# One multiplication and one sum for the dots of four gathered rows, in one group of three

## The reference

```python
qry = (xb @ peer_query).reshape(P, PEER_HEADS, 2, PEER_KEY_DIM)
scores = jnp.einsum('phsd,hsnd->phsn', qry, keys)
top_s, top_i = lax.top_k(scores, PEER_TOPK)
cand = top_s[:, :, 0, :, None] + top_s[:, :, 1, None, :]
best_s, best_c = lax.top_k(cand.reshape(...), PEER_TOPK)
expert = ia * PEER_KEYS + ib            # 16 experts per frame and head
gate = jax.nn.softmax(best_s)
act = jax.nn.gelu(jnp.einsum('pd,ped->pe', xb, peer_down[expert]))
out = jnp.einsum('pe,ped->pd', gate * act, peer_up[expert])
```

## Time and profile before

| | |
|---|---|
| time, median of 3 runs | 1663.01 us (1662.77 to 1663.81) |
| profiled execution, time | 1664.46 us |
| its span, first to last instruction | 1662.7 us |
| busy: TensorE, VectorE, ScalarE, GpSimd | 1383.8, 1174.9, 573.3, 716.7 us |
| DMA | 608.39 MB, mean 366 GB/s |
| mean granted TensorE clock | 0.946 |

### The profile page before, as it was taken

The page is one execution under the profiler, slowest core; times in us unless marked ns, Lnnn a source line. Parts: engine busy times, 40 slices in busy tenths (PEclk is TensorE's granted clock), DMA queues, the critical chain, the costliest instruction groups (busy, mean ns, idle before and its releaser), DMA issues.

```text
span 1662.7 us, 14018 instructions
## 1 busy us (share of the span) xinstructions
PE 1383.8 (83%) x4311; PEld 678.6 (41%) x4311; DVE 1174.9 (71%) x2555; ACT 573.3 (34%) x1785; POOL 716.7 (43%) x633
## 2 busy tenths in 40 slices
PE   7999999998898789778977897789779877777733
PEld 6744465554353335324433443344324423332311
DVE  3997758966876777677767776777777777676755
ACT  3112231632433333333333333333433333333342
POOL 0004624644444445444444444445444444444552
PEclk9999999999899999999999999999999999999955
DMA  7203227999999999999999999999999999999996
GB/s 293 102 1 100 110 77 279 371 421 422 422 420 422 421 422 420 422 421 422 420 422 421 422 421 422 421 421 421 421 422 421 421 422 420 419 420 421 414 421 256
DMA packets 87978, 608.39 MB, mean 366 GB/s; under 512 B 11104, under 2 KB 13664, under 8 KB 16224
## 3 DMA queue, kind: packets, MB, share of 16 engines
q0 software_dynamic: 78336, 570.46, 82.9%
q1 hardware_dynamic: 9568, 37.04, 5.9%
HBM read 604.19 MB, written 2.88 MB: 365 GB/s over the span
## 4 chain that ended last, share of the span: by engine, by line
DMA 44%; PE 37%; DVE 10%; issue 3%; ACT 3%; POOL 2%; DVEq 0%; SPq 0%; POOLq 0%
DMA arena<-experts,expert 44%; PE ps L1686 18%; PE ps L1549 8%; PE ps L1649 5%; DVE arena L1329 4%; PE ps L1529 4%; POOL arena L603 2%; ACT weight L907 1%; ACT late L917 1%; PE ps L1508 1%; DVE cst L1305 0%; DVE cst L1308 0%; DVE picked L1312 0%; PE ps L1620 0%; ACT gl L899 0%
## 5 line engine op out<-in xcount | busy, mean ns | idle before, releaser
L1686 PE MATMUL ps<-arena,late 128*128 128x512 f32 x2016 | 950.3, 624 | 206.0 <-ACT late L917 205.7
L603 POOL DMA_INDIRECT arena<-experts,expert x544 | 645.2, 1186 | 732.4 <-PE ps L1686 627.5
L1329 DVE CUSTOM_DVE_ANT_0 arena<-arena,hn 128x1024 f32<-128x1024 f32 x544 | 656.7, 1222 | 384.9 <-DMA arena<-experts,expert 381.8
L1686 PEld LDWEIGHTS ps<-arena,late 128*128 128x128 f32 x2016 | 387.3, 198 | 745.0 <-issue 450.7
L899 ACT ACTIVATE gl<-dots 128x2 f32<-128x2 f32 (+1 forms) x274 | 55.8, 204 | 814.3 <-DVE dots L1329 814.3
L917 ACT ACTIVATE late<-cst,weight 128x128 f32<-128x128 f32 (+1 forms) x536 | 183.5, 389 | 8.8
L907 ACT ACTIVATE weight<-gl,gate 128x1 f32<-128x1 f32 x544 | 130.7, 287 | 8.9
L1549 PE MATMUL ps<-arena,hT 128*128 128x512 f32 x256 | 112.3, 598 | 0.0
L1649 PE MATMUL ps<-hT,region_b 128*128 128x272 f32 x448 | 106.9, 392 | 0.0
L1649 PEld LDWEIGHTS ps<-hT,region_b 128*128 128x128 f32 x448 | 85.1, 190 | 27.9 <-issue 12.4
L1072 DVE SCALAR_TENSOR_TENSOR region_b<-region_b,par 128x574 f32<-128x574 f32 x120 | 92.5, 813 | 4.5
(11 more groups left out here) (174 smaller groups left out, 872.1 us busy)
## 6 DMA issues: line engine op xcount, KB each, us to landing
arena<-weights SPq DMA_DIRECT2D x6, 2048.0 KB, 11.0
region_b<-head_weights SPq DMA_DIRECT2D x8, 1152.0 KB, 9.5
arena<-experts,expert POOLq DMA_INDIRECT x544, 22.4
hT<-x_turned SPq DMA_DIRECT2D x2, 1088.0 KB, 7.2
arena<-weights SPq DMA_DIRECT2D x4, 512.0 KB, 10.7
xs<-x_prompt SPq DMA_DIRECT2D x4, 512.0 KB, 10.0
arena<-weights SPq DMA_DIRECT2D x2, 1024.0 KB, 13.9
y_prompt<-xs SPq DMA_DIRECT2D x4, 512.0 KB, 3.8
```

Of the source, the lines that this page charges most:

```text
L603: pool.indirect_dma_start(rows_of(n), None, experts, bass.IndirectOffsetOnAxis(ap=expert[:, vt % BUFS, k:k + 1], axis=0))\
L1329: last = v.tensor_tensor_reduce(out=rows_of(n)[:, 0:D], in0=rows_of(n)[:, 0:D], in1=hn[:, tile_of(vt)], scale=1.0, scalar=0.0, op0=ALU.mul ...
L1686: last = mm(ps[:, 2 * (vt % 2) + half, :], diag[:, n % DIAGS, :], rows_of(n)[:, D + half * SEC:D + (half + 1) * SEC], start=k == first * G ...
```

## The change

Three things are changed. The last four slots of `CYCLE` come in the order 10, 11, 8, 9, whose places are 0, 1, 2, 3. `FOURS` lists the groups, between rows 64 and 511, whose four buffers lie side by side in that order: every third group, 38 in all, beginning with row 64, 76, 88 and so on to 508. By visit they are the first and the fourth group of visits 4, 7, 10 ..., the third of 5, 8, 11 ..., the second of 6, 9, 12 .... Their gathers count on one common semaphore, `s_four`. For such a group VectorE waits for all four rows, multiplies the four down rows with the frame's row in one instruction of 4096 elements (in place), and sums them to four dots in a second one, which then signals for both pairs.

```diff
-CYCLE = [2, 3, 6, 4, 5, 0, 1, 7, 8, 9, 10, 11]
+CYCLE = [2, 3, 6, 4, 5, 0, 1, 7, 10, 11, 8, 9]
...
-TURN = [SLOT[:n + 1].count(slot) for n, slot in enumerate(SLOT)]
+FOURS = [n for n in range(4 * TOPK, (VT - 2) * TOPK, GROUP)
+         if [PLACE[SLOT[n + k]] - PLACE[SLOT[n]] for k in range(GROUP)] == [0, 1, 2, 3]]
+FOUR = {n + k: i + 1 for i, n in enumerate(FOURS) for k in range(GROUP)}
+TURN = [sum(m not in FOUR and SLOT[m] == slot for m in range(n + 1)) for n, slot in enumerate(SLOT)]
...
-                        .then_inc(s_slot[SLOT[n]], 16)
+                        .then_inc(s_four if n in FOUR else s_slot[SLOT[n]], 16)
...
+            def weigh_four(vt, first):
+                dve.wait_ge(s_four, 16 * GROUP * FOUR[first])
+                here = PLACE[SLOT[first]]
+                downs = ring_rows[:, here:here + GROUP, 0:D]
+                ranked(v.tensor_tensor(out=downs, in0=downs,
+                                       in1=hn[:, tile_of(vt)].unsqueeze(1).to_broadcast([P, GROUP, D]), op=ALU.mult))
+                dve.wait_ge(s_ranked, len(ranks))
+                k = first - vt * TOPK
+                v.tensor_reduce(out=dots[:, vt % 2, k:k + GROUP], in_=downs, axis=AX.X, op=ALU.add)\
+                    .then_inc(s_dot, sum(n in DOTTED for n in range(first, first + GROUP)))
+
             def weigh(vt, g):
+                first = vt * TOPK + g * GROUP
+                if first in FOUR:
+                    weigh_four(vt, first)
+                    return
```

More of the change, by code:

```diff
@@ L417, in build @@
         s_slot = [sem(f"s_slot{i}") for i in range(SLOTS)]
+        s_four = sem("s_four")
         s_dot = sem("s_dot")
```

## The result

| | before | changed |
|---|---|---|
| time, median of 6 runs | 1663.69 us (1662.77 to 1665.25) | 1671.20 us (1668.61 to 1674.38) |
| ratio, 95% interval | | 1.0045 (1.0034 to 1.0056) |
| profiled execution: time, span | 1664.46, 1662.7 us | 1672.51, 1670.7 us |
| mean granted TensorE clock | 0.946 | 0.907 |

The changed kernel is slower by 7.5 us, 0.45%. That lies inside the stated range, but outside the 0.2% around no change where the forecast of 1665.3 us stood. It is the side of rival (b).

What follows compares the result with a forecast made beforehand. The DMA stream of gathered rows at 421 GB/s was taken as the bound. One 2.3 us dry queue in head 1, all else zero, gave 1666.8 us profiled, 1665.3 us at the median; range 1662.3 to 1674.

Steps and rivals of the forecast that it cites:

- rival (b): Query visits, heads 1 and 4: a longer chain starves the queue; total 4.6 us, up to 9.5; chance 0.30.
- the store of 19 to 22 us: DMA queue: time from a gather's issue to its landing, 22.5 us at the median, 19.2 at least; expected to hide the edit.
- The two places: First tiles of heads 1 and 4, with queries and two big groups: a late start is not made up there.
- 162 us more on VectorE: VectorE, all 38 groups: added occupation from the dearer pair, which stays under the DMA and costs nothing by itself.
- The durations: VectorE, each big group: product and sum at 4.40 us each, the pair 8.85 us, up to 11.1.
- The chain from landing to the next pass: Big groups: pair 8.85, 1.24 to first matmul, half clock 2.2, then 2.2 us to the gather reusing the buffer.
- x: Extra us in the chain from landing to matmul beyond the reckoned length; loss steps at 0.5, 1.7, 2.2 and 2.9.
- The port: GpSimd, head 1: gather 94 waits out the big multiplication and lands late, leaving the queue dry for 2.3 us.
- the reckoning of gather 92: Head 1: gather 92 starts at 501.6 us and would land at 507.1, due 507.5, so no loss.
- rival (a): Head 1: gather 94 passes before the multiplication, or lands 3.5 us after its start; no loss, 1663.0 us; chance 0.23.
- The margin of 2.9 us at unhurried groups: 36 of 38 groups: the first row's new gather lands at 27.0 us, due at 29.9, so cost zero.
- Rival (c): All 38 big groups starve the queue once the chain is 2.9 us longer; 42 us at 4 us longer; chance 0.09.

Runs made afterwards that it cites:

- e1: Kernel before with only the new order of the last four slots of CYCLE, all dots single: 1663.79 us, ratio 0.9996.
- e3: Changed kernel with 34 of the 38 big groups; those of rows 64, 76, 256 and 268 get single dots: 1662.85 us, ratio 0.9990.
- e9: Changed kernel with each big group's sum made in two halves, the first two dots signalled 2.2 us sooner: 1662.41 us, ratio 0.9988.
- e5: Changed kernel whose 38 groups still wait for four landings, then make four old fused dots instead of product and sum: 1664.96 us, ratio 0.9997.
- e4: Changed kernel with the product of 128x4096 cut into four of 128x1024, the single sum kept: 1674.03 us, ratio 1.0050.
- e10: Changed kernel with one more reduction of 1024 elements before the sum, so dots come 1.3 us later: 1696.50 us, ratio 1.0186.
- e6: Changed kernel with query pieces of 2 matmuls instead of 16: 1667.71 us, ratio 1.0020.
- e2: Changed kernel with only four big groups, those of rows 64, 76, 256 and 268: 1666.57 us, ratio 1.0009.

## Why the prediction was off

**What bounds the kernel, and the question asked** were right. The DMA's stream sets the time, the change lengthens the hold of a buffer, and the store of 19 to 22 us was the thing to watch; it fell to 11 (some 15 was reckoned). The two places were right, heads 1 and 4, and so were the zero cost of the order (e1), of the 162 us more on VectorE (e3, e9) and of the wait by itself (e5).

**The durations** were right: 4.43 and 4.42 against 4.40 us.

**The chain from landing to the next pass** was the term that was mis-sized. In head 1:

- landing to the first matmul: 457.62 - 447.35 = 10.27, reckoned 8.85 + 1.24 = 10.1;
- the group's matmuls: 467.46 - 457.62 = 9.84 at a granted clock of 0.71, which is 2.97 over 6.87; for the half clock 2.2 was taken, with bounds from 1.7 to 3.4;
- from a row's first matmul to the gather of the next pass: 2.66 (471.12 to 473.78), reckoned 2.2;
- in all, gather 80 starts 26.4 us after the landing of row 67, reckoned 10.1 + 10.53 + 2.2 + 2.2 = 25.0.

So x = 1.4 (0.2 before the matmuls, 0.8 in them, the rest at the gather), within the bounds given for rival (b): loss in both heads, in the profile 3.3 + 3.2 us. Between the steps at x = 0.5 and x = 1.7, (b) gave 4.6 us; the medians have 5.7 and 7.5. Rival (b), at 0.30, had the right places and the right ground, a chain longer than reckoned. Its prices were wrong all the same: they were holds of gathers 94 and 286 by the port, and both took 0.94 us. That 4.6 lies near the measured loss is partly luck. In the forecast no term stood at its late bound, and when the start is late they all move that way.

**The port** was the step that failed. It was said to turn gather 94's hold into a dry queue for 2.3 us. In the trace gather 94 escapes (508.31, 0.94 us) and 95 is held (4.73 us), but row 95 lands only 0.3 us late; e4, with no gather over 2 us in the 200 us shown, gains nothing, and e9, with the holds, loses nothing. And the delay came a pass earlier, at gathers 81 and 82, which the reckoning of gather 92 had passed over: it followed one pass too far, since it took the store at the first pass for sure. With x = 1.4, gather 80 lands 26.4 + 6.1 = 32.5 us after row 67, and due is 13 x 2.49 = 32.4. That is the edge for rows 80 and 81, in one line; the 1.7 us of row 82, whose gather was issued 10.4 us before the row landed, no such reckoning gives. That the total of 2.3 us in head 1 by row 91 is the number forecast is chance. (Under rival (a), a held gather that lands 3.5 us after its start would by the prediction's own figures still be 0.3 us late, not in time.)

**The margin of 2.9 us at unhurried groups** held in that the 34 others cost nothing (e3), and failed as a number: 1.3 us more would not have mattered, and did, 24 us (e10). Its mean was well reckoned and its spread left out: in the changed kernel the gather that reuses the first buffer of a big group starts 21.8 us after that row's landing at the median (21.5 were reckoned), but 23.4 to 27.1 in nine of 37 groups, and the edge was reckoned at 24.4. With 1.3 us more (e10) the median is 23.4. Rival (c) would have been next, far sooner than at x = 2.9.

**What stays open:** the half of the loss that e6 keeps without query work; why row 82 landed 4.2 us after row 81 although its gather had been issued 1.2 us after the other's, with the DMA engines counted as busy; what part of the loss, if any, the port has; what part of the executions of e2 have the loss; and why e9 is below the kernel before.

## What to carry to other kernels

Where a stream of transfers sets the time, price a batched operation by when its first result comes and by how long each buffer is held, against what stands queued for the DMA. Follow the chain at the first visit where a late start can't be made up, with each term at its late bound, and look at the spread of the margin, not at its mean. Hand on the first half of a batch as soon as it is there (e9): the batch may stay. And measure the margin by adding a known delay (e10) before calling an edit free.

## What the runs showed of the hardware that was not expected

- GpSimd's issue of a gather can be stretched from 0.94 to 4.97 us by one VectorE product of 128x4096 with both inputs in SBUF (in the page its mean rose from 1186 to 1336 ns), and by itself that cost nothing (e9 keeps the holds at a ratio of 0.9988; e4 has none over 2 us and loses as much as the changed kernel).
- The mean DMA rate between 400 and 1500 us was 417 GB/s in e3 and 416 in the changed kernel, with no loss in one and 6 to 7 us in the other.
- A sum of 128x4096 is as dear as a product of it, 4.42 us, and cutting it in two costs 2.29 + 2.28 = 4.57.
- A stretch of TensorE in part at half clock behind 10 to 14 us of idling cost 1.6 us (e5, granted clock 0.82) to 3.0 (changed kernel, 0.70) in a group of 16 matmuls, and no time of the kernel in e5.
- With few rows queued (row 82 on its way, head 1 of the changed kernel), the DMA engines counted as busy (share 0.98 to 1.00) and moved 287 to 324 GB/s for 4 us, where a full stream has 421 at a share of 1.01.
